# First layer's shared projections dealt into its attention and level steps by an order table; probabilities transposed unscaled

## The reference, cut to what matters

```python
(a_q, a_k, a_v, a_g, g_q, g_k, g_v, g_af, g_ab, g_g,
 s_u, s_v, s_g, m_a, m_g, m_s) = jnp.split(h @ p['w_in'], pts, axis=-1)
...
def attend(q, k, v):                       # 8 heads of 64, 2 key heads
    s = einsum('btgrd,blgd->bgrtl', q, k) * (64 ** -0.5)
    p = softmax(s, axis=-1)
    return einsum('bgrtl,blgd->btgrd', p, v)
y_attn = blocked_attention(ql, k_all, v_all) * silu(a_g)
# gated linear attention: decays b = cumsum(log_sigmoid(z)/16), both directions
att = einsum('bhtd,bhsd,bhtsd->bhts', qc, kc, exp(rel))   # rel = b_t - b_s
o = inter + einsum('bhts,bhse->bhte', att, vc)
y_sgu = s_u * (w_s @ layer_norm(s_v) + b_s) * silu(s_g)
```

## Time and profile before

| | us |
|---|---|
| median of three runs | 1471.01 (1470.66 to 1472.67) |
| the profiled execution's own time | 1467.76 |
| span of its profile | 1466.0 |
| PE busy | 1352.9 (92%) |
| DVE busy | 650.2 (44%) |
| ACT busy | 505.0 (34%) |
| granted TensorE clock, mean | 0.966 of full |

### The profile page before, as it was taken

How to read it: one execution, slowest core, us unless ns; L and a number is a source line. 1 busy time by engine, 2 the same in 40 slices (tenths; PEclk the granted TensorE clock), 3 DMA queues, 4 the chain that set the end, 5 groups by cost and what they waited for, 6 DMA issues and landing times. The chain is left out here.

```text
span 1466.0 us, 19469 instructions
## 1 busy us (share of the span) xinstructions
PE 1352.9 (92%) x8018; PEld 1028.2 (70%) x8018; DVE 650.2 (44%) x1197; ACT 505.0 (34%) x840; POOL 44.6 (3%) x36
## 2 busy tenths in 40 slices
PE   6999897688999999998998979999999989999996
PEld 2787576466678888887975658999776656666663
DVE  2322364777223434457736784566622342222222
ACT  2224431434352323234453546444135221111112
POOL 0000000211000000002000020000000000000000
PEclk7999999889899999999999999999999999999998
DMA  9422210213512234322431201565233558999990
GB/s 388 193 86 87 86 58 29 105 69 115 230 58 87 87 106 181 109 85 101 150 140 58 86 2 59 177 226 175 101 115 115 243 230 336 410 406 403 422 377 31
DMA packets 34223, 238.98 MB, mean 163 GB/s; under 512 B 4304, under 2 KB 4432, under 8 KB 6224
## 3 DMA queue, kind: packets, MB, share of 16 engines
q1 hardware_dynamic: 34128, 237.66, 42.1%
HBM read 236.59 MB, written 1.05 MB: 162 GB/s over the span
## 5 line engine op out<-in xcount | busy, mean ns | idle before, releaser
L229 DVE TENSOR_TENSOR pieces_lo<-weight_ring,pieces_hi 128x1024 fp32r<-128x1024 f32 x154 | 187.5, 1223 | 319.5 <-ACT pieces_hi L221 319.4
L247 PE MATMUL proj<-h_hi,pieces_hi 128*128 128x512 f32 (+1 forms) x816 | 287.2, 352 | 8.3 <-DVE h_lo L1127 2.9
L249 PE MATMUL proj<-h_hi,pieces_lo 128*128 128x512 f32 (+1 forms) x816 | 282.3, 346 | 0.0
L248 PE MATMUL proj<-h_lo,pieces_hi 128*128 128x512 f32 (+1 forms) x816 | 281.3, 345 | 0.0
L221 ACT ACTIVATE pieces_hi<-weight_ring 128x1024 fp32r<-128x1024 f32 x158 | 165.7, 1053 | 132.9 <-PE proj L249 69.2
L247 PEld LDWEIGHTS proj<-h_hi,pieces_hi 128*128 128x128 f32 x816 | 154.2, 189 | 36.6 <-issue 8.7
L248 PEld LDWEIGHTS proj<-h_lo,pieces_hi 128*128 128x128 f32 x816 | 154.9, 190 | 21.7 <-issue 1.4
L249 PEld LDWEIGHTS proj<-h_hi,pieces_lo 128*128 128x128 f32 x816 | 154.2, 189 | 20.5
L1917 PE MATMUL turn<-expert_parts,e_gathered 128*64 128x256 f32 x768 | 85.3, 379 | 0.8 <-DVE e_gathered L2106 0.8
L1917 PEld LDWEIGHTS turn<-expert_parts,e_gathered 128*64 128x64 f32 x768 | 56.0, 137 | 32.4 <-issue 7.3
L761 PE MATMUL turn<-l_diag,l_probs 128*128 128x128 f32 x320 | 48.7, 309 | 29.6 <-DVE l_diag L1191 14.3
(11 more groups left out here) (433 smaller groups left out, 1998.3 us busy)
## 6 DMA issues: line engine op xcount, KB each, us to landing
weight_ring<-in_stream SPq DMA_DIRECT2D x110, 1024.0 KB, 4.8
expert_parts<-in_experts SPq DMA_DIRECT2D x70, 1024.0 KB, 10.9
weight_ring<-in_experts SPq DMA_DIRECT2D x26, 1024.0 KB, 10.7
l_rows<-in_rows SPq DMA_DIRECT2D x2, 768.0 KB, 15.6
l_y_attn<-in_ada_first SPq DMA_DIRECT2D x1, 1024.0 KB, 5.0
l_y_gla<-in_ada_first SPq DMA_DIRECT2D x1, 1024.0 KB, 7.1
l_y_sgu<-in_ada_first SPq DMA_DIRECT2D x1, 1024.0 KB, 8.0
l_q<-in_ada_first SPq DMA_DIRECT2D x1, 1024.0 KB, 9.8
```

The lines of the kernel that those rows point to most:

```text
L229: eng.tensor_tensor(self.part(self.lo_ring[:, n % NPIECE, :], kind), self.raw(slot, c, kind), self.part(self.hi_ring[:, n % NPIECE, :], ki ...
L247: pe.matmul(out, sh, mh, start=start, stop=False)
L248: pe.matmul(out, sh, ml, start=False, stop=False)
L249: return pe.matmul(out, sl, mh, start=False, stop=stop)
```

## The change

1. Layer 0's list is now `first` (the `ada`, `h` and `hsplit` steps) followed by a table written out word by word, `ORDER_0`. The front begins with `ag`. The eight pieces of `sg` and `su` leave it: `sg` stands around units 3 to 6, `su` between level steps. `gv` stands between `rot` and `decay` steps, `sv` between the key steps, `ada` steps one by one.
2. `sg` of layer 0 is copied out by ACT as it is, and one `sgsilu` step does the SiLU of all four tiles at once.
3. Both layers: `turn` is a PE transpose of the unscaled probabilities and waits only for the exponential. `sums` is one DVE reciprocal per unit. `pv` gets one more PE product per head, which spreads the reciprocals over the partitions, and one more DVE multiplication. `score` stands before the `sums` of the unit before.
4. Both layers: `decay`, `diag`, `key` and `svn` are cut in two steps each (`decay.0/1`, `diag.0/1`, `key`/`keymul`, `svstat`/`svn`). In layer 1 the halves follow one another.

```diff
+ORDER_0 = """
+ag.0 ag.1 ag.2 ag.3 ak.0 gq.0 gq.1 gate.0 aq.0 z.0 aq.1 z.1 aq.2 z.2 aq.3 z.3 stat.0 gk.0 stat.1 stat.2 gk.1
+stat.3 stat.4 soft.0 av.0 rstd.0 rstd.1 rstd.2 rstd.3 rstd.4 gv.0 rot.0 rot.1 gv.1 rot.2 rot.3 decay.0 rot.4
+vt.0 decay.1 gv.2 score.0 key.0 gv.3 keymul.0 score.1 sums.0 turn.0 sv.0 keyt.0 key.1 sv.1 keymul.1 ada.0.4
+adat.0.4 sums.1 turn.1 sv.2 keyt.1 kv.0 kv.1 sv.3 kv.2 svstat.0 svn.0 score.2 pv.0 score.3 sg.0 sums.2 diag.0
+turn.2 pv.1 sg.1 score.4 diag.1 sums.3 turn.3 sg.2 pv.2 diff.0 score.5 sums.4 sg.3 turn.4 scale.0 diff.1 pv.3
+score.6 sgsilu.0 sums.5 scale.1 pairs.0 diff.2 turn.5 pv.4 su.0 score.7 scale.2 pairs.1 diff.3 sums.6 turn.6
+ada.0.5 adat.0.5 pv.5 scale.3 pairs.2 diff.4 score.8 sums.7 mix.0 turn.7 scale.4 pairs.3 diff.5 pv.6 score.9
+su.1 sums.8 scale.5 pairs.4 diff.6 ada.1.0 turn.8 adat.1.0 pv.7 score.10 scale.6 pairs.5 diff.7 sums.9 mix.1
+su.2 turn.9 pv.8 scale.7 pairs.6 diff.8 score.11 sums.10 turn.10 scale.8 pairs.7 diff.9 pv.9 ada.1.1 adat.1.1
+score.12 sums.11 scale.9 pairs.8 diff.10 turn.11 mix.2 pv.10 score.13 scale.10 pairs.9 diff.11 sums.12 su.3
+turn.12 pv.11 scale.11 pairs.10 diff.12 score.14 ada.1.2 adat.1.2 sums.13 turn.13 scale.12 pairs.11 diff.13
+pv.12 mix.3 score.15 sums.14 scale.13 pairs.12 turn.14 ada.1.3 adat.1.3 pv.13 sums.15 pairs.13 turn.15 ada.1.4
+adat.1.4 pv.14 pv.15 query.0 ada.1.5 adat.1.5
+"""
...
-        first += [(n, i) for n in ("sg", "su", "ag") for i in range(4)]
+        steps = first + [named(word) for word in ORDER_0.split()]
...
-            att += [s for s in (("sums", i - 1), ("score", i), ("turn", i - 1), ("pv", i - 2)) if 0 <= s[1] < n_units]
+            att += [s for s in (("score", i), ("sums", i - 1), ("turn", i - 1), ("pv", i - 2)) if 0 <= s[1] < n_units]
...
                 elif kind == "turn":
-                        pe.wait_ge(*sig.probs.at(2 * i + u + 1))
+                        pe.wait_ge(*PS.evacuated(J("score", i, u)))
...
-                            last = pe.matmul(acc[:, b * P:(b + 1) * P], PR[:, i % 2, u, b * P:(b + 1) * P], diag[:, u, :],
-                                             start=True, stop=True)
+                            last = pe.transpose(acc[:, b * P:(b + 1) * P], PR[:, i % 2, u, b * P:(b + 1) * P], ident)
...
+                    pe.wait_ge(*sig.inverse.at(i + 1))
+                    for u in range(2):
+                        last = pe.matmul(acc[64 * u:64 * u + 64, P:2 * P], inverse[:, i % 4, u:u + 1].to_broadcast([P, 64]), ident,
+                                         start=True, stop=True)
...
+                elif kind == "sg" and l == 0:
+                    act.wait_ge(*PJ.ready(J("sg", i)))
+                    act.activation(YS[:, i, :], PJ.tile(J("sg", i))[:, :], ACT.Copy).then_inc(*PJ.evac(J("sg", i)))
+                elif kind == "sgsilu":
+                    for k in range(4):
+                        act.wait_ge(*PJ.evacuated(J("sg", k)))
+                    act.activation(YS[:], YS[:], ACT.Silu).then_inc(*sig.sg_silu.one())
...
                 elif kind == "sums":
                     for u in range(2):
                         dve.wait_ge(*PS.evacuated(J("score", i, u)))
-                        if i:
-                            dve.wait_ge(*PT.ready(J("turn", i - 1, u)))
-                        link(dve.reciprocal(small[:, i % 2, 6 + u:7 + u], small[:, i % 2, 4 + u:5 + u]))
-                        dve.tensor_scalar(diag[:, u, :], ident, small[:, i % 2, 6 + u:7 + u],
-                                          None, ALU.mult).then_inc(*sig.probs.one())
+                    dve.reciprocal(inverse[:, i % 4, :], small[:, i % 2, 4:6]).then_inc(*sig.inverse.one())
...
-                    dve.tensor_tensor(YA[:, j, tok:tok + P], PJ.tile(J("pv", i))[:, 0:P], YA[:, j, tok:tok + P],
-                                      ALU.mult).then_inc(*PJ.evac(J("pv", i)))
+                    y = YA[:, j, tok:tok + P]
+                    link(dve.tensor_tensor(y, PJ.tile(J("pv", i))[:, P:2 * P], y, ALU.mult))
+                    dve.tensor_tensor(y, PJ.tile(J("pv", i))[:, 0:P], y, ALU.mult).then_inc(*PJ.evac(J("pv", i)))
```

More of the change, by code:

```diff
@@ L289, in __init__ @@
         self.inverse = signal("inverse_sums")
+        self.sg_silu = signal("sg_silu")
         self.keys = signal("keys")
@@ L396, in with_splits @@
         if m < NPIECE:
-            at = steps.index(("ada", ADA_ORDER[2]) if m < 2 else ("sg", 0)) if early else 0
+            at = steps.index(("ada", ADA_ORDER[2]) if m < 2 else steps[use[0][0]]) if early else 0
         pieces.plan(slot, c, kind, engine, c == PIECES_OF_SLOT.get(slot[2:], 4) - 1)
@@ L407, with named @@
 ADA_ORDER = [(0, n) for n in ADA_FIRST + (4, 5)] + [(1, n) for n in range(6)]
+ORDER_0 = """
[13 more added lines that the diff above has]
+"""
+def named(word):
+    name, *at = word.split(".")
+    return name, int(at[0]) if len(at) == 1 else tuple(map(int, at))
 def trunk_schedule(l):
@@ L432, in trunk_schedule @@
[L432 to L455, removed]
+        first += [("ak", 0), ("gq", 0), ("gq", 1), ("gate", 0)]
@@ new lines, in trunk_schedule @@
+        first += [("aq", 0), ("z", 0), ("aq", 1), ("z", 1), ("aq", 2), ("z", 2), ("aq", 3), ("z", 3)]
+        first += [("stat", 0), ("gk", 0), ("stat", 1), ("stat", 2), ("gk", 1), ("stat", 3), ("stat", 4), ("soft", 0), ("av", 0)]
+        rot = [("rstd", i) for i in range(5)] + [("rot", i) for i in range(5)] + [("vt", 0), ("decay", 0), ("decay", 1)]
+        gv, sv = ([(n, g) for g in range(4)] for n in ("gv", "sv"))
+        att = []
+        for i in range(n_units + 2):
+            att += [s for s in (("score", i), ("sums", i - 1), ("turn", i - 1), ("pv", i - 2)) if 0 <= s[1] < n_units]
@@ new lines, in trunk_schedule @@
+        halves = 2 * len(LEVELS)
+        levels = [[s for s in (("scale", n - 1), ("pairs", n - 2), ("diff", n)) if 0 <= s[1] < halves] for n in range(halves + 2)]
+        rest = [("key", 0), ("keymul", 0), gv, ("keyt", 0), ("key", 1), ("keymul", 1)]
+        rest += [sv + [("svstat", 0), ("svn", 0)], ("keyt", 1), ("kv", 0), ("kv", 1), ("kv", 2), ("diag", 0), ("diag", 1)]
+        fill = [("mix", g) for g in range(4)]
+        for n, r in enumerate(levels):
+            rest += r
+            if n % 2 and fill:
+                rest.append(fill.pop(0))
@@ L456, in trunk_schedule @@
+        rest += [("query", 0)]
+        steps, done = first + rot, 0
+        for n, a in enumerate(att):
+            steps.append(a)
+            upto = (n + 1) * len(rest) // len(att)
+            steps += sum((r if type(r) is list else [r] for r in rest[done:upto]), [])
+            done = upto
     steps += [("ysplit", ("s", k)) for k in range(4)] + [("gg", 0), ("gg", 1), ("silu", 0), ("silu", 1), ("out", 0), ("out", 1)]
@@ L505, in trunk_layer @@
     first_use = ("z", 0)
+    first_dense = ("ag", 0) if l == 0 else ("sg", 0)
     units = units_of(l)
@@ L521, in trunk_layer @@
         ada_row = YG[:, 3, :]
-        diag = sb("diag", [P, 2, P])
+        inverse = sb("inverse_sums", [P, 4, 2])
         stats = sb("stats", [P, 4, 16])
@@ L807, in _ @@
                         q, k = DQ, DK
[L809 to L817, removed]
+                    p = i % 2
+                    acc = [PJ.open(pe, J(kind, i, u)) for u in range(2)]
+                    for c in range(C0, NCH):
+                        for u in range(2):
+                            last = pe.matmul(acc[u][:, (c - C0) * P:(c - C0 + 1) * P],
+                                             k[64 * u:64 * u + 64, p, c * P:(c + 1) * P],
+                                             q[64 * u:64 * u + 64, p, c * P:(c + 1) * P], start=True, stop=True)
+                            if c == NCH - 1:
+                                last.then_inc(*PJ.done())
                 elif kind == "mix":
@@ L1240, in _ @@
                     elif i > 1:
-                        dve.wait_ge(*PJ.ready(J("pairs", i - 2, p, 1)))
+                        dve.wait_ge(*PJ.ready(J("pairs", i - 2, 1)))
                     f, b, q, k = (half_views(x, p, h) for x in (BF, BB, DQ, DK))
```

45 lines of the change are left out of this document (23 added, 22 removed).

## The result

| | before | after |
|---|---|---|
| median, us | 1470.84 (4 runs, 1469.01 to 1472.67) | 1457.82 (4 runs, 1455.92 to 1459.92) |
| span of the profile, us | 1466.0 | 1455.5 |
| granted clock, mean | 0.966 | 0.966 |

What follows compares the result with a forecast made beforehand. PE, busy 92%, was taken as the bound, so time comes only from its waits, half clock or dropped work. 44.5 + (84 - 86) + (129 - 123) + 6 = 54.5 us off gave 1416 us, range 1394 to 1441.

Steps and rivals of the forecast that it cites:

- The front: Layer 0 up to the end of `av`: loses eight pieces of 5.56 us and nothing else, 44.5 us off.
- From `av` to the first `diff`: Layer 0 before the levels: 84 us become 86, of which PE's part is 80; bounds 80 and 94.
- From the first `diff` to `gg`: Layer 0's levels: 129 us become 123, from 96 of PE work plus waits; bounds 103 and 147.
- The term for `ada`: In the levels, PE stands about 2.7 us seven times because `ada` is copied behind a `diff`'s exponential: 19 us.
- The forms: Both layers' new `turn`, `sums`, `pv`: layer 0's `turn` work 21.2 to 10.6 us, spreading adds 4.8, `l_diag` waits go.
- Layer 1: Layer 1's attention: less `turn` work and no `l_diag` waits, 6 us shorter; bounds 0 and 10.5.
- The sum: Whole kernel: 44.5 + (84 - 86) + (129 - 123) + 6 = 54.5 us gained.
- PE dense: Rival: the `ada` waits in the levels vanish, last part 103 us, total 1396 us; chance 0.18.
- Half clock: Rival: PE runs at 1.2 GHz through the mixed stretch, slower than before, up to 1559 us; chance 0.04.
- Interlock: Rival: DVE stands through the new pieces between the levels, last part 147 us, total 1440 us; chance 0.26.
- Nothing comes of it: Rival: the stretch after the front grows by the 44.5 us that the front loses; chance 0.02.
- The rule on transposes: Counter-rule for the mixed stretch: its 96 transposes could leave more of it at 1.2 GHz; a profile row spoke against it.

Runs made afterwards that it cites:

- e3: The changed kernel with layer 0's `score.2` moved ahead of `svstat.0` and `score.3` behind `sg.0`; 1453.70 us.
- e2: The kernel before with only the new forms of `turn`, `sums` and `pv`, old order in both layers; 1457.77 us.
- e1: The changed kernel with layer 1's list in the order of before, its steps cut in two in place; 1442.66 us.
- e6: The changed kernel with layer 1's old order, `score.2` ahead of `svstat.0`, `score.3` behind `sg.0`, `key.0` behind `gv.3`, `ada.0.4` and `adat.0.4` apart; 1434.51 us.
- e9: The changed kernel with layer 1's `score.1` moved behind `gv.3`; 1454.45 us.
- e10: The changed kernel with layer 1's `score.1` moved behind `gv.3` and `score.2` behind `kv.0`; 1446.96 us.

## Why the prediction was right or wrong

**The front**: right. 43.3 of 44.5 us (173 to 129.7), at a clock of 1.00 from 41 us on, with the weight stream's new order at no cost that the trace shows. The missing 1.2 us lie at the start, where the half clock lasted to 39.6 us (31.0 in before) and the first `ag` piece took 8.5 us.

**From `av` to the first `diff`: the step that failed.** "I walked the table through the queues ... I take 86 us", with 80 us of PE at full clock and some 5 us of waits. Measured 108.7: PE was busy 53.1 + 37.5 = 90.5 us, and stood for 18.2. Both terms were too small. Of the waits I had 1 us before `score.0`, 1 at `ada`, 3 behind `sv.3`; there were 3.1 for the copies of `gv`, 2.2 for DVE's use of `adat`, 5.4 for the bank of `pv.0`, which is the last of mine mis-sized, and 4.5 for `score.3`, which I had not seen at all: I followed `pv.0` through `svn`, but not the minimum of `score.2`, which stands behind the same `svn` on DVE. e3 moved `score.3` and `score.2` and won 4.1 us by the medians, and 7.3 from the first score to the first `pairs` by the profiles. The other term is PE's work, 10.5 us above my 80. The half clock is 6.8 of them, by the three rows above. Another 2.4 are the price of a piece: one that stands between small steps takes 5.78 us at full clock until the next step starts, 11 times 0.22 more than the 5.56 that I had from the earlier trace rows. The last 1.3 are in the small steps. I had the earlier trace rows with 0.90 for the same stretch of before and still priced PE at full clock, and the bound of 94 us held the old waits but no clock.

**From the first `diff` to `gg`**: 123 predicted, 125.7 measured, but partly by two errors that cancel. PE was busy 107 us instead of 96, and its waits were 18 us instead of 27. Of the 11 us 6.5 are half clock, for which the 96 had nothing: 13.7 us of the stretch were at 1.2 GHz, with PE at work for 13.0. The term for `ada`, 19 us, was 16.1. That DVE would stand through the `su` pieces only for a small part was right, 1.9 us each instead of 1.3:

```profile
DVE l_y_sgu L1170 <- PE proj L249: 7.6, 4, 2.9
```

**The forms**: right in kind. e2 shows them at 13 us, 9.9 of them in layer 0, where the prediction had them inside its floor and the 8.4 us for `l_diag`, and 5.4 in layer 1.

**Layer 1: the second step that failed.** "Bounds 0 and 10.5; I take 6" was made for an unchanged order. I read that the halves follow one another, and did not work through the rule that deals the list, although the exchange of `score` and `sums` stood in the change; it put two scores ahead of work that doesn't need them. Measured: 9.7 us lost. With the old order (e1) the forms gave 5.2. Without this step the time would still be above the range's end of 1441, at e1's 1442.66; this step alone, 15.7 us on top of 1416.5, would have stayed inside it.

**The sum.** 22.7 us in the first failed step, 15.7 in the second, 2.7 in the levels, 1.2 in the front and 2.2 in the mixer are 44.5, against 54.5 - 10.5 = 44.0 between the predicted and the profiled gain.

**The rivals.** *PE dense* and *Half clock* did not come. *Interlock* had the right sign but the wrong place: it put its 24 us into the levels, where they did not arise. *Nothing comes of it*, at 0.02, was nearest to the time, and in layer 0 it was half right: of the 43.3 us off the front the steps up to `gg` gave 21 back. No rival had a cost in layer 1, so the range stopped at 1441.

**The rule on transposes.** The Trainium skill, "TensorE: Matmul & The Clock Gate", Part 4, says that the full clock does not engage for transpose mode. It did not show itself here, as the earlier trace rows had said. e2 has the transposes in place of the products in an unchanged order, and nearly the granted clock of before, 0.84 against 0.85:

```profile
257.00:386.00 129.00, 104.47 (x845) 69.58 (x836) 80.64 (x186) 52.70 (x106) 21.55 (x14) 0.84 0.36 139
```

In after two of the three slow pieces, `sv.0` and `sv.2`, do stand behind transposes, but a wait is there as well (3.1 and 2.2 us). e6 has the same transposes ahead of `sv.0` and a shorter wait, and there the piece, from 161.4 us on, has the full clock (the wait, then the stretch of the piece):

```profile
PE proj L247 <- ACT x_context L1002: 1.4, 1, 1.4
```

```profile
161.40:167.30 5.90, 5.88 (x26) 4.75 (x27) 2.24 (x5) 2.73 (x8) 0.00 (x0) 1.00 0.47 178
```

So the half clock of `sv.0` goes with the wait and not with the transposes.

## What to carry to other kernels

Where one list sets the order of all queues, print the list of every layer before and after an edit and compare them word by word: exchanging two steps in one of two lists that a rule interleaves, and adding three entries to the other, moved steps in a layer whose order had looked untouched, and cost more than the new order elsewhere won. For each step ask on every engine what long work stands ahead of it, not only on the engine where the step waits; a `score` is PE work of 1 us, but its bank hangs on DVE's queue, behind 8 us of scans or 6 us of normalisation. And where the profile of before shows 0.90 in a stretch, price new work there at that clock, not at that of the front.

## What the runs showed of the hardware

The same instructions in the same order do not take the same time in each profile. The levels of layer 0, first to last `pairs`, took 106.0 us in after, 105.9 in e1, 110.2 in e9 and 111.0 in e10, which differ only in layer 1. After and e10 have granted clocks of their own, 0.94 and 0.87, between 244 and 352 us:

```profile
244.00:352.00 108.00, 92.67 (x766) 67.43 (x765) 70.91 (x162) 46.89 (x87) 17.16 (x13) 0.94 0.28 108
```

```profile
244.00:352.00 108.00, 93.16 (x711) 67.80 (x709) 70.70 (x160) 45.72 (x85) 17.22 (x14) 0.87 0.25 98
```

There is one profile for each kernel, so whether this belongs to the kernel or to the single execution is open. The executions of one kernel do differ: e1's four went from 1438.97 to 1446.81 us. What decides was not found. In the stretches shown here the half clock comes at or behind a wait of PE, and in the levels there is always another wait. The spread is as large as most single moves in the list, and it is why the gain of one such move (e3's 4.1, e6's 0) should be read from its own waits first, and from the medians with care.
